# Values times probabilities of the band heads: from f32 products per query tile to three f32r passes per key tile

## What is computed

```python
def softmax_attend(q, k, v, bias):
    s = jnp.einsum('...qhd,...khd->...hqk', q, k).astype(jnp.float32) * (HEAD_DIM ** -0.5) + bias
    p = jax.nn.softmax(s, axis=-1)
    return jnp.einsum('...hqk,...khd->...qhd', p.astype(v.dtype), v)

z = rmsnorm(x, g_attn) @ w_in
q_a, k_a, v_a, q_m, x_b, g_b = jnp.split(z, SPLITS, axis=-1)
...
x = x + jnp.concatenate([o_a, o_m, o_b], axis=-1) @ w_out
up = rmsnorm(x, g_ffn) @ w_up
...
x = x + (jax.nn.gelu(gt) * val) @ w_down
```

## Time and profile before

| | us |
|---|---|
| median of 3 runs (2325.09 to 2325.97) | 2325.2 |
| the profiled execution | 2325.38 |
| its span, from the first to the last instruction | 2323.6 |
| PE busy | 2314.1 (100%) |
| PE weight loads busy | 2285.7 (98%) |
| DVE busy | 1745.2 (75%) |
| ACT busy | 1117.6 (48%) |
| POOL busy | 307.5 (13%) |

### The profile page before, as it was taken

The page is one execution under the profiler, slowest core; times in us unless marked ns, Lnnn a source line. Parts: engine busy times, 40 slices in busy tenths (PEclk is TensorE's granted clock), DMA queues, the critical chain, the costliest instruction groups (busy, mean ns, idle before and its releaser), DMA issues.

```text
span 2323.6 us, 44878 instructions
## 1 busy us (share of the span) xinstructions
PE 2314.1 (100%) x18088; PEld 2285.7 (98%) x18088; DVE 1745.2 (75%) x2302; ACT 1117.6 (48%) x1756; POOL 307.5 (13%) x258
## 2 busy tenths in 40 slices
PE   9999999999999999999999999999999999999999
PEld 8999999999999999999999999999999999999999
DVE  6777555554424798888888888888888988786876
ACT  4555343333322455545554555555555555454543
POOL 5100000000022112112111121111111110000000
PEclk9999999999999999999999999999999999999999
DMA  9522323332533344344434344343444678686864
GB/s 294 148 83 76 110 82 88 90 95 82 178 110 104 91 131 140 116 120 126 126 112 139 111 140 117 117 131 121 120 131 135 178 200 203 158 208 158 215 146 102
DMA packets 479141, 309.88 MB, mean 133 GB/s; under 512 B 10840, under 2 KB 457176, under 8 KB 478952
## 3 DMA queue, kind: packets, MB, share of 16 engines
q1 hardware_dynamic: 470520, 289.97, 42.4%
q0 software_dynamic: 8432, 17.27, 4.6%
HBM read 255.79 MB, written 53.51 MB: 133 GB/s over the span
## 4 chain that ended last, share of the span: by engine, by line
PE 94%; DVE 3%; DMA 1%; issue 1%; ACT 0%; SPq 0%; POOL 0%; DVEq 0%; ACTq 0%; POOLq 0%
PE out L2531 21%; PE out L2533 21%; PE out L2532 20%; PE out L2177 9%; PE out L2178 9%; PE out L2180 9%; PE out L2188 2%; PE out L2328 1%; PE out L2271 1%; PE out L2286 1%; DVE ring_l L1851 1%; DMA out_yT<-stage 0%; DVE fl L2085 0%; PE out L2370 0%; ACT ring_h L1314 0%
## 5 line engine op out<-in xcount | busy, mean ns | idle before, releaser
L1851 DVE TENSOR_TENSOR ring_l<-pair,ring_h 128x1024 fp32r<-128x1024 f32 (+1 forms) x384 | 455.8, 1187 | 177.8 <-ACT ring_h L1314 177.7
L1314 ACT CAST ring_h<-pair 128x1024 fp32r<-128x1024 f32 (+1 forms) x384 | 383.0, 998 | 321.4 <-DVE pair L1878 227.7
L2531 PE MATMUL out<-t,ring_h 128*128 128x272 f32 x1536 | 443.8, 289 | 1.2 <-DVE ring_l L1851 0.6
L2533 PE MATMUL out<-t,ring_l 128*128 128x272 f32 x1536 | 444.2, 289 | 0.0
L2177 PE MATMUL out<-xh,wh 128*128 128x272 f32 x1600 | 443.6, 295 | 0.0
L2532 PE MATMUL out<-t,ring_h 128*128 128x272 f32 x1536 | 441.9, 288 | 0.0
L2178 PE MATMUL out<-xl,wh 128*128 128x272 f32 x1600 | 431.4, 288 | 0.0
L2531 PE MATMUL out<-fh,ring_h 128*128 128x272 f32 x1344 | 387.7, 288 | 2.8 <-DVE ring_l L1851 2.1
L2533 PE MATMUL out<-fh,ring_l 128*128 128x272 f32 x1344 | 387.5, 288 | 0.0
L2532 PE MATMUL out<-fl,ring_h 128*128 128x272 f32 x1344 | 386.2, 287 | 0.0
L2531 PE MATMUL out<-b_forms,ring_h 128*128 128x272 f32 x1152 | 331.7, 288 | 0.0
(11 more groups left out here) (260 smaller groups left out, 3847.2 us busy)
## 6 DMA issues: line engine op xcount, KB each, us to landing
pair<-in_w_up SPq DMA_DIRECT2D x192, 512.0 KB, 4.0
raw<-in_w_in SPq DMA_DIRECT2D x36, 1024.0 KB, 5.6
pair<-in_w_down SPq DMA_DIRECT2D x64, 384.0 KB, 4.1
pair_d<-in_w_down SPq DMA_DIRECT2D x64, 384.0 KB, 4.6
h_forms<-fb SPq DMA_DIRECT2D x24, 816.0 KB, 6.0
fr<-h_forms SPq DMA_DIRECT2D x24, 816.0 KB, 7.3
out_yT<-stage POOLq DMA_DIRECT2D x31, 544.0 KB, 8.0
raw<-in_w_out SPq DMA_DIRECT2D x16, 1024.0 KB, 5.8
```

The lines of the kernel that those rows point to most:

```text
L1314: nc.scalar.copy(ring_h[:, n % 3, 0:width(i)], weight_of(p, i)).then_inc(op_hi, 1)
L1851: v.tensor_tensor(ring_l[:, n % 3, 0:w], weight_of(p, i), ring_h[:, n % 3, 0:w].bitcast(F32), ALU.subtract).then_inc(op_lo, 1)
L2531: mm(out, w_high, high[:, k, :], start=opens and k == 0, stop=False, skip_group_check=True)
L2533: ins = mm(out, w_low, high[:, k, :], start=False, stop=k == tiles - 1, skip_group_check=True)
```

## The change

Where the prompt's values and probabilities of a band head are read from `flip`, they are split as the projections' operands are: ACT writes the high part in f32r (`v_high`, `prob_high`) and raises a new semaphore `turned_high`; DVE waits for that, subtracts the high part from the same bank (`v_low`, `prob_low`) and raises `flip_read`. DVE's new steps are `low_v` in beat 1, between the logits and the division, and `low_prob` in beats 3 to 6, at the end of `head`. The sample rows and the outputs are read as before.

The transposed probabilities are laid out by key tile: key tile c has its query tiles c to 3 side by side. A read of query tile t thus writes t + 1 blocks in different places, in one instruction for one or two blocks and in two for three or four (`turned`). PE's output becomes, for each of four key tiles, three passes over all its query tiles: high values x high probabilities, high x low, low x high, of 512, 384, 256 and 128 columns, all added in the one bank.

The new buffers lie over ones that are dead by then (`v_rows`, `memv`, `probT`, and `rg` with `xb`). `x_again` goes: the second reading of `xT` counts on `x_in` too, and DVE waits for 32 instead of 16.

```diff
+        def turned(t):
+            at = (0, 3 * P, 5 * P, 6 * P)
+            for c in range(0, t + 1, 2):
+                n = min(2, t + 1 - c)
+                step = at[c + 1] - at[c] if n > 1 else P
+                yield flip[:, c * P:(c + n) * P].rearrange("p (b n) -> p b n", n=P), at[c] + t * P, n, step
+        def key_block(buf, c):
+            at = (0, 4 * P, 7 * P, 9 * P)[c]
+            return buf[:, at:at + (Q_TILES - c) * P]
...
-                if t < Q_TILES:
+                if t < Q_TILES and a < HM:
                     n = keys(a, t)
                     nc.scalar.copy(probT[:, at:at + n], flip[:, 0:n]).then_inc(flip_read, 1)
+                elif t < Q_TILES:
+                    for src, *where in turned(t):
+                        ins = nc.scalar.copy(blocks(prob_high, *where), src)
+                    ins.then_inc(turned_high, 1)
...
-                    nc.scalar.copy(v_rows[:, 0:Q_TILES, :],
-                                   flip.rearrange("p (t n) -> p t n", n=P)).then_inc(flip_read, 1)
+                    nc.scalar.copy(v_high[:], flip.rearrange("p (t n) -> p t n", n=P)).then_inc(turned_high, 1)
...
+            def low_v(h, more):
+                dve.wait_ge(turned_high, TILES * h + 1 + TILES * more)
+                nc.vector.tensor_tensor(v_low[:], flip.rearrange("p (t n) -> p t n", n=P),
+                                        v_high[:].bitcast(F32), ALU.subtract).then_inc(flip_read, 1)
+            def low_prob(h, t, more):
+                dve.wait_ge(turned_high, TILES * h + t + 2 + TILES * more)
+                for src, *where in turned(t):
+                    ins = nc.vector.tensor_tensor(blocks(prob_low, *where), src,
+                                                  blocks(prob_high, *where).bitcast(F32), ALU.subtract)
+                ins.then_inc(flip_read, 1)
             def head(a, beat, more=0):
                 if beat < TILES:
                     logits(a, beat, more)
+                if a >= HM and beat == 1:
+                    low_v(a - HM, more)
                 if 1 <= beat <= TILES:
                     probs(a, beat - 1, more)
+                if a >= HM and 3 <= beat < 3 + Q_TILES:
+                    low_prob(a - HM, beat - 3, more)
...
+                        for c in range(Q_TILES):
+                            out, high, low = flip[:, c * P:SEQ], key_block(prob_high, c), key_block(prob_low, c)
+                            mm(out, v_high[:, c, :], high, start=c == 0, stop=False, skip_group_check=True)
+                            mm(out, v_high[:, c, :], low, start=False, stop=False, skip_group_check=True)
+                            ins = mm(out, v_low[:, c, :], high, start=False, stop=c == Q_TILES - 1,
+                                     skip_group_check=True)
...
-                    dve.wait_ge(x_again[m // 4], 16)
+                    dve.wait_ge(x_in[m // 4], 32)
```

More of the change, by code:

```diff
@@ L188, in encoder @@
         memk = place(at_a, "memk", [P, HM, N_MEM])
+        v_low_at = overlay + at_a[0]
         memv = place(at_a, "memv", [P, HM, 2, P])
+        probT_at_a = overlay + at_a[0]
         probT = place(at_a, "probT", [P, 10 * P + 2 * DEC])
@@ L193, in encoder @@
         kT = place(at_a, "kT", [P, ROWS])
+        v_rows_at = overlay + at_a[0]
         v_rows = place(at_a, "v_rows", [P, TILES, P])
@@ L199, in encoder @@
         past = place(at_a, "past", [P, 2, 4, P])
+        prob_low_at = overlay + at_a[0]
         rg = place(at_a, "rg", [P, 2, RT, P])
@@ L213, in over @@
             return nc.alloc_sbuf_tensor_at(name, shape, dt, offset=offset)
+        v_high = over("v_high", [P, Q_TILES, P], v_rows_at, F32R)
+        v_low = over("v_low", [P, Q_TILES, P], v_low_at, F32R)
+        prob_high = over("prob_high", [P, 10 * P], probT_at_a, F32R)
+        prob_low = over("prob_low", [P, 10 * P], prob_low_at, F32R)
+        assert 4 * 10 * P <= 4 * (2 * RT * P + ROWS + 2 * (CB - 1))
         form = K8 * HALF * 4
@@ L294, in encoder @@
         x_in = [sem(f"x_in{n}") for n in range(4)]
-        x_again = [sem(f"x_again{n}") for n in range(4)]
         table_in = sem("table_in")
@@ L331, in encoder @@
         flip_read = sem("flip_read")
+        turned_high = sem("turned_high")
         k_out = sem("k_out")
@@ L424, in probT_at, with blocks @@
             return t * (t + 1) // 2 * P
+        def turned(t):
[4 more added lines that the diff above has]
+                yield flip[:, c * P:(c + n) * P].rearrange("p (b n) -> p b n", n=P), at[c] + t * P, n, step
+        def blocks(buf, at, n, step):
+            return buf[:, at:at + n * step].rearrange("p (b n) -> p b n", n=step)[:, :, 0:P]
+        def key_block(buf, c):
+            at = (0, 4 * P, 7 * P, 9 * P)[c]
+            return buf[:, at:at + (Q_TILES - c) * P]
         def mem_bank(t):
@@ L700, in _ @@
                 sp.dma_start(rows[:, 4 * n:4 * n + 4, :],
-                             k_major(xT)[:, 4 * n:4 * n + 4, :]).then_inc(x_again[n], 16)
+                             k_major(xT)[:, 4 * n:4 * n + 4, :]).then_inc(x_in[n], 16)
             def spill(k):
@@ L2322, in output @@
                 if s == 0:
[L2323 to L2329, removed]
+                    if a < HM:
+                        for t in range(Q_TILES):
+                            n = keys(a, t) // P
+                            for c in range(n):
+                                at = probT_at(a, t) + c * P
+                                ins = mm(flip[:, t * P:(t + 1) * P], memv[:, a, c, :], probT[:, at:at + P],
+                                         start=c == 0, stop=c == n - 1)
+                    else:
+                        for c in range(Q_TILES):
[4 more added lines that the diff above has]
+                                     skip_group_check=True)
                 else:
```

## The result

| | before | after |
|---|---|---|
| median | 2325.3 us (6 runs) | 2344.0 us (6 runs, 2343.8 to 2344.2) |
| profiled execution | 2325.4 | 2344.2 |
| span | 2323.6 | 2342.4 |

The ratio is 1.008, with a 95% interval of 1.0067 to 1.0093: slower by 18.7 us, where 21.3 us were forecast. The forecast was 2346.5 us in a range of 2334 to 2354.

A forecast was written before the change was run, and what follows sets the result against it. PE's own queue was taken as the bound. Stalls of 24.0 us less 2.7 us gained in the product gave 21.3 us more: span 2344.9, profiled time 2346.7, median 2346.5 us, range 2334 to 2354.

The forecast's parts named there:

- The bound and the places: PE's queue bounds the band heads; DVE's late release makes it wait before tile 2's and the sample rows' transposes.
- the five contents: Bank `flip` per head: values, query tiles 0 and 2 released in time; tiles 1 and 3 released late by DVE.
- The first stall: PE waits before tile 2's transposes for tile 1's subtraction, behind DVE's queue up to tile 3's division: 1.73 us a head.
- The second stall: PE waits before the sample rows' transposes for tile 3's subtraction, behind DVE's normalisation of q: 1.59 us a head.
- Head 7: No `read_z` or normalisation on DVE there, so only a stall of 0.78 us, after tile 1's subtraction.
- The product: PE's output block per head: twelve f32r passes in 1.90 us instead of 2.235, a gain of 2.7 us over eight heads.
- the two stalls are nearly independent: Without the wait before tile 2, the one before the sample rows would be 1.75 us instead of 1.59.
- the clock rival: PE's clock falls to 1.2 GHz for one beat after each of 15 stalls: 50 us more, 2397 us; chance 0.03.
- In time: DVE reaches tiles 1 and 3 before PE wants them, leaving only the gain: 2322.5 us; chance 0.06.
- One stall only: A reading error at one of the two places leaves a single stall a head: about 2335 us; chance 0.08.
- Dearer low parts: DVE's block-wise subtractions cost twice the assumed price: 8 us more, 2355 us; chance 0.08.
- The narrow passes run as four: PE's 128-column f32r passes take as long as f32 ones, so the product saves nothing: 2349.2 us; no separate chance given.

The follow-up runs named there:

- the long wait: The kernel with both low parts moved ahead, plus an idle 570-column reciprocal on DVE ahead of tile 3's low part in heads 0 to 6: 2345.6 us.

## Why the prediction was right

*The bound and the places.* Right. PE's queue was full, so each wait counted whole; the two places, the releaser, and the five contents in time or late are as the working said. Both moves of a step show it: with tile 3's ahead, seven waits go; with both, all.

*The first stall*, 1.73 us: 1.57. Tile 1's subtraction began at 304.08, 0.09 before the end of the division, and PE's matmul 0.05 behind its end (304.50), where I had taken 0.15 from the earlier trace rows and no overlap. *The second stall*, 1.59: 1.44. From tile 2's transposes to the square root I had 2.45 us, and it was 2.44; from there to the end of the subtraction 5.88 against 5.79; the time at which PE was due had moved by 0.05. So the chain was right and its joints were up to 0.1 us too wide, nearly all in the same direction. *Head 7*, 0.78: an idle row of 0.54 us, 0.7 us from start to start. Together 7 x 3.01 + 0.7 = 21.8 us where 24.0 were summed: 2.2 us of a miss of 2.5.

*The product.* 1.90 us a head forecast, 1.925 measured, with 0.115 for a narrow pass against 0.05, 0.12 and 0.11. That it is so near is partly luck: the narrow passes took 0.28 us instead of 0.345, the wider ones 1.59 instead of 1.554, and the second matmul behind the block came 0.055 us late, for which the sum had no term. 8 x 0.31 = 2.5 us against 2.7.

*The sum.* 21.8 - 2.5 = 19.3 us, which is how far the changed kernel was behind at the end of head 7's product. The span grew by 18.8: the 0.5 us are the wait at 1871.78 in the kernel before, of which the prediction had nothing. So the miss of 2.5 us is 2.2 of stalls and 0.5 of that wait, less 0.2 of the product. Head periods (304.55 to the same row of the next heads, 352.05 and 399.67) are 47.5 and 47.6 us, forecast 47.8.

*What was wrong.* The sentence that the two stalls are nearly independent, with 1.75 us for the second without the first. It changed nothing in the forecast, which has both. As the first wait was taken away here, the second was 2.5 us: the first stall had let ACT and DVE catch up, and the move delayed what the square root waits for. And the clock rival: with a chance of 0.03 and a loss after every wait, it was rightly not chosen for this kernel, but the ground given against it, an idle row of 1.29 us at full clock, says nothing of a wait of 2.2 us.

*The rivals.* In time: shown to be what a better order gives (2322.6, forecast 2322.5, with 0.7 us of the gain from the wait at 1871.78), not what this order gives. One stall only: both were there. Dearer low parts: 0.42 us for 256 columns and 0.75 for two of them, as priced. The narrow passes run as four: excluded, as a pass of 128 columns took 0.11 us.

## What to carry to other kernels

Before a release moves from one engine to another, write down what stands in the new engine's in-order queue at that moment, not how busy it is: before the change DVE was idle for 43% of a head, and it was still late twice. Where that queue has long steps, put the release ahead of them; the same steps in another order turned +18.7 us into -3 us. And splitting an f32 product into three f32r passes paid here only with passes of up to 512 columns: in pieces of 128 it took 11.5 us more.

## What the runs showed of the hardware

- Waits of PE with idle rows up to 1.4 us cost their length and no clock. With idle rows of 2.0 to 2.4 us the granted clock fell to 1.2 GHz in or behind 13 of 21: two of seven in the run with tile 3's subtraction twice, five with tile 1 ahead, six with the long wait. Each fall cost about 1.6 us more (0.93 instead of 1.00 over 23 us). Two waits of 1.4 us, 8 us apart, did not lower it. By the Trainium skill ("TensorE: Matmul & The Clock Gate", "What's actually happening") the clock follows how busy the array was; the traces agree, and show that a mostly busy kernel can lose it too.
- An f32r pass, start to start: 0.23 us at 512 columns, 0.18 at 384, 0.117 at 256, 0.11 at 128, and a first narrow one of 0.05 to 0.06.
- PE's first matmul came 0.15 us after DVE's end in nine of the fifteen waits (312.78 to 312.93), and 0.05 us in the other six, those before tile 2 in heads 1 to 6 (304.50 to 304.55). The same transposes in heads 0 and 7 had 0.15 us, so it isn't their shape; what it is stays open.
- ACT's table load ahead of the square root took 1.28 us.
